# Modulation matrix of a two-layer hybrid diffusion block: one group ahead of the input projection, five through a ring beside attention, in unsplit fp32 products

## What is computed

```python
def reference(x, c, ctx, c_ctx, ada_w, ada_b, norm_w, ...):
    sc, scc = jax.nn.silu(c), jax.nn.silu(c_ctx)
    xc = ctx
    for layer in range(DEPTH):                    # DEPTH = 2
        m = jnp.split((sc @ ada_w[layer] + ada_b[layer])[:, None, :], 6, axis=-1)
        mc = jnp.split(scc @ ada_w[layer] + ada_b[layer], 6, axis=-1)
        nw = norm_w[layer]
        h = modulate(rmsnorm(x, nw[0]), m[0], m[1])       # h * (1 + scale) + shift
        hc = modulate(rmsnorm(xc, nw[0]), mc[0], mc[1])
        y, yc = even_mixer(h, hc, ...) or odd_mixer(h, hc, ...)
        x = x + m[2] * rmsnorm(y, nw[1])
        x = x + m[5] * rmsnorm(ffn(modulate(rmsnorm(x, nw[2]), m[3], m[4])), nw[3])
        # the same for xc with mc, in the first layer alone
    return x
```

## Time and profile before

| what | us |
|---|---|
| median of three runs | 2601.38 |
| lowest, highest | 2595.45, 2602.39 |
| span of the profiled execution | 2596.3 |
| modulation with its columns | 0 to 173.2 |
| norm, up to the first product of the projection | 173.2 to 198.5 |
| input projection | 198.5 to 366 |
| attention jobs | 366 to 476 |

### The profile page before, as it was taken

How to read it: one execution, slowest core, us unless ns; L and a number is a source line. 1 busy time by engine, 2 the same in 40 slices (tenths; PEclk the granted TensorE clock), 3 DMA queues, 4 the chain that set the end, 5 groups by cost and what they waited for, 6 DMA issues and landing times. The chain is left out here.

```text
span 2596.3 us, 29102 instructions
## 1 busy us (share of the span) xinstructions
PE 2334.5 (90%) x11454; PEld 1842.6 (71%) x11454; DVE 1607.9 (62%) x1534; ACT 1205.4 (46%) x1247; POOL 241.4 (9%) x200
## 2 busy tenths in 40 slices
PE   5979999799976999897897759999999999999995
PEld 1338855589865888786755647888888887888884
DVE  5972238453474222233437657888888888888884
ACT  4642222322223222223314326777677777777763
POOL 0000028032410000000034100000000000000000
PEclk9989986899988999998888869999999999999998
DMA  8962210000012333122200128999999999999993
GB/s 316 379 234 80 92 40 1 15 1 1 1 66 78 85 97 98 49 97 97 83 1 1 65 98 304 355 360 348 360 337 361 349 358 330 359 349 345 363 356 128
DMA packets 254976, 482.51 MB, mean 186 GB/s; under 512 B 11314, under 2 KB 80107, under 8 KB 254587
## 3 DMA queue, kind: packets, MB, share of 16 engines
q1 hardware_dynamic: 254703, 478.59, 52.5%
q0 software_dynamic: 144, 2.10, 0.2%
HBM read 479.57 MB, written 1.08 MB: 185 GB/s over the span
## 5 line engine op out<-in xcount | busy, mean ns | idle before, releaser
L134 DVE TENSOR_TENSOR arena_r<-arena,arena_r 128x2048 fp32r<-128x2048 f32 (+2 forms) x466 | 958.5, 2068 | 334.4 <-ACT arena_r L130 314.9
L130 ACT ACTIVATE arena_r<-arena 128x2048 fp32r<-128x2048 f32 (+2 forms) x466 | 804.4, 1737 | 355.0 <-DMA arena<-in_moe_w 272.6
L2009 PE MATMUL bank<-arena_r,gate_rows_r 128*128 128x512 f32 x896 | 350.6, 391 | 0.0
L139 PE MATMUL bank<-hT_r,arena_r 128*128 128x512 f32 (+2 forms) x656 | 254.4, 388 | 37.0 <-DVE arena_r L134 37.0
L2007 PE MATMUL bank<-arena_r,arena_r 128*128 128x512 f32 x672 | 267.0, 397 | 0.0
L2008 PE MATMUL bank<-arena_r,arena_r 128*128 128x512 f32 x672 | 261.5, 389 | 0.0
L140 PE MATMUL bank<-catT_r,arena_r 128*128 128x512 f32 (+2 forms) x656 | 253.8, 387 | 0.0
L141 PE MATMUL bank<-hT_r,arena_r 128*128 128x512 f32 (+2 forms) x656 | 253.4, 386 | 0.0
L2043 PE MATMUL bank<-arena_r,hT_r 128*128 128x512 f32 x448 | 185.7, 414 | 11.6 <-DVE catT_r L2187 11.6
L2009 PEld LDWEIGHTS bank<-arena_r,gate_rows_r 128*128 128x128 f32 x896 | 169.0, 189 | 36.3
L2044 PE MATMUL bank<-arena_r,hT_r 128*128 128x512 f32 x448 | 175.5, 392 | 0.0
(11 more groups left out here) (361 smaller groups left out, 3626.3 us busy)
## 6 DMA issues: line engine op xcount, KB each, us to landing
arena<-in_moe_w SPq DMA_DIRECT2D x336, 1024.0 KB, 5.3
arena<-in_ada_w SPq DMA_DIRECT2D x48, 1024.0 KB, 5.3
arena<-in_ffn_w SPq DMA_DIRECT2D x44, 512.0 KB, 5.2
arena<-in_ev_w_in SPq DMA_DIRECT2D x14, 1024.0 KB, 5.3
arena<-in_ffn_w SPq DMA_DIRECT2D x11, 1024.0 KB, 4.8
arena<-in_od_w_in SPq DMA_DIRECT2D x9, 1024.0 KB, 5.2
arena<-in_ev_w_out SPq DMA_DIRECT2D x4, 1024.0 KB, 8.6
arena<-in_od_w_out SPq DMA_DIRECT2D x4, 1024.0 KB, 8.1
```

Source lines behind the costliest of these rows:

```text
L130: return act.activation(rounded(hi), v, ACT.Copy)
L134: return dve.tensor_tensor(rounded(v), v, rounded(hi).bitcast(F32), ALU.subtract)
L139: pe.matmul(acc, xh_, wh_, start=start, stop=False)
L2009: mm = pe.matmul(out_bank, lo, wh[:, k, :], start=False, stop=(kk == KD - 1))
```

## The change

The six parts of each layer's matrix are taken as three groups of 2048 columns, so six groups of 8 MB in all, each in eight slots of 128 rows by 2048 columns (1 MB). Group 0 is loaded into the arena ahead of the input projection and multiplied there. The other five go through three buffers in `G` (`RING`): three loads are issued at the end of the projection, and 37 beside the attention, each after the product that frees its buffer. Splitting is dropped: a slot is multiplied in plain fp32, in four products of 512 columns whose outputs lie in partitions 0 to 31, 32 to 63, 64 to 95 and 96 to 127 of bank 7. The stationary operand is padded with zeros to 32 columns. VectorE adds the bias rows (`stage`), TensorE turns the whole bank with four transposes, and VectorE writes `modc` and the gate rows of the group. In the attention the eight slots of a group follow jobs 6n to 6n + 4 (two, two, two, one, one), and the turns job 6n + 5. Between two groups SP also writes the gate rows and loads the next bias and norm rows. The first norm's squares, scaling and 28 of its turns are moved ahead of group 0's products; the gate rows are spread into `G` during a later block. The constants are loaded behind seven small loads, and x and ctx ahead of the matrix.

```diff
-        NSLOT, NCH = 6, 24
-        AW = [cut(i * 2048, 4, 512) for i in range(NSLOT)]
-        AWH = ([cut((NSLOT + i) * 2048, 4, 512) for i in range(2)] + [hT[:, 2:6, :]]
-               + [G[:, 2 * i:2 * i + 2, :].rearrange("p a (b n) -> p (a b) n", b=2) for i in range(3)])
...
+        ONE = 2048
+        FIRST = [cut(k * ONE, ONE) for k in range(KD)]
+        RING = [G[:, 2 * i:2 * i + 2, :].rearrange("p a n -> p (a n)") for i in range(3)]
+        GROUPS = [(l, g) for l in range(2) for g in range(3)]
+        n_deferred = (len(GROUPS) - 1) * KD
+        MODS = {0: ((0, 0), (1, 1)), 1: ((1, 2),), 2: ((0, 3),)}
+        GATES = {1: (0, 1, 0), 2: (1, 3, 1)}
+        stage, abias, anorm = sb("ada_stage", [P, 512]), sb("ada_bias_rows", [P, 512]), sb("ada_norm_rows", [P, 512])
+        scP = small[:, 384:640].rearrange("p (k m) -> p k m", k=KD)
...
+        def ada_load_slot(sp, m):
+            n, k = divmod(m, KD)
+            l, g = GROUPS[n + 1]
+            if m >= 3:
+                sp.wait_ge(s_au, KD + m - 2)
+            sp.dma_start(RING[m % 3], adaw[l][:, k, g * ONE:g * ONE + ONE]).then_inc(s_ring[m % 3], 16)
...
+        def ada_store_gates(sp, n):
+            l, g = GROUPS[n]
+            if g in GATES:
+                half, _, which = GATES[g]
+                sp.wait_ge(s_mg, ada_gates_made(n))
+                for jj in range(2):
+                    j = 2 * half + jj
+                    sp.dma_start(gate_dram[l, which, :, jj * 512:jj * 512 + 512], stage[32 * j:32 * j + 2, :]).then_inc(s_g_out, 16)
+
+        def ada_product(pe, slot, k):
+            for j in range(4):
+                mm = pe.matmul(bank[7][32 * j:32 * j + 32, :], scP[:, k, :], slot[:, 512 * j:512 * j + 512], start=(k == 0), stop=(k == KD - 1))
+            mm.then_inc(s_au, 1)
+
+        def ada_slot(pe, m):
+            n, k = divmod(m, KD)
+            if k == 0:
+                pe.wait_ge(s_am, n + 1)
+            pe.wait_ge(s_ring[m % 3], 16 * (m // 3) + 16)
+            ada_product(pe, RING[m % 3], k)
+
+        def ada_turn(pe, n):
+            pe.wait_ge(s_ast, n + 1)
+            for b in range(4):
+                mm = pe.transpose(bank[7][:, b * P:b * P + P], stage[:, b * P:b * P + P], ident)
+            mm.then_inc(s_at, 1)
+
+        def ada_stage_rows(dve, n):
+            dve.wait_ge(s_au, KD * (n + 1))
+            dve.wait_ge(s_ab, ada_bias_landed(n))
+            if n and ada_gates_made(n - 1):
+                dve.wait_ge(s_g_out, 32 * ada_gates_made(n - 1))
+            dve.tensor_tensor(stage[:, :], bank[7][:, :], abias[:, :], ALU.add).then_inc(s_ast, 1)
...
+        def ada_cols(dve, n):
+            l, g = GROUPS[n]
+            dve.wait_ge(s_at, n + 1)
+            turned = bank[7][:, :].rearrange("p (m j c) -> p j m c", m=4, j=4)
+            for half, j in MODS[g]:
+                of = turned[:, 2 * half:2 * half + 2, :, :]
+                if j % 2 == 0:
...
+            ins.then_inc(s_am, 1)
+            if g in GATES:
+                dve.tensor_tensor(stage[:, :], stage[:, :], anorm[:, :], ALU.mult).then_inc(s_mg, 1)
+
+        n_group_jobs = 6
+        ada_slots_at = {n_group_jobs * n + d: [KD * n + s for s in ss]
+                        for n in range(len(GROUPS) - 1) for d, ss in enumerate(((0, 1), (2, 3), (4, 5), (6,), (7,)))}
+
+        def ada_pe_beside(pe, it):
+            for m in ada_slots_at.get(it, ()):
+                ada_slot(pe, m)
+            n, d = divmod(it, n_group_jobs)
+            if d == n_group_jobs - 1 and n + 1 < len(GROUPS):
+                ada_turn(pe, n + 1)
+
+        def ada_dve_beside(dve, it):
+            n, d = divmod(it, n_group_jobs)
+            if n + 1 < len(GROUPS):
+                if d == n_group_jobs - 2:
+                    ada_stage_rows(dve, n + 1)
+                elif d == n_group_jobs - 1:
+                    ada_cols(dve, n + 1)
+
+        def ada_sp_beside(sp):
+            for m in range(3, n_deferred):
+                ada_load_slot(sp, m)
+                n, k = divmod(m - 2, KD)
+                if k == KD - 1:
+                    ada_store_gates(sp, n + 1)
+                    if n + 2 < len(GROUPS):
+                        sp.wait_ge(s_ast, n + 2)
+                        ada_load_bias(sp, n + 2)
+            ada_store_gates(sp, len(GROUPS) - 1)
...
+        def load_in(sp, c):
+            sp.dma_start(WR[c % NWR], WIN[:, :, c * 256:c * 256 + 256]).then_inc(s_wi0[c % NWR], 16)
...
                 sp.dma_start(X[:, 2:4, :], t["ctx"].rearrange("(t p) d -> p t d", p=P)).then_inc(s_x, 16)
+                for k in range(KD):
+                    sp.dma_start(FIRST[k], adaw[0][:, k, 0:ONE]).then_inc(s_first[k], 16)
+                    if k == 3:
+                        sp.wait_ge(s_zero, 1)
+                        ada_load_bias(sp, 0)
+                for c in range(NWR):
+                    load_in(sp, c)
+                sp.dma_start(wg[:, :, :], WIN[:, :, 3584:3600]).then_inc(s_wg, 16)
...
-                def chunk(i, first):
-                    for s in range(NSLOT):
-                        b, h = divmod(s, 2)
-                        if not first and h == 0:
-                            pe.wait_ge(s_row, 3 * i + (b - 2))
-                        pe.wait_ge(s_al, NSLOT * i + (s + 1))
-                        for k in range(4):
-                            kk = 4 * h + k
-                            mm = split_matmul(pe, bank[b][0:2, :], (scTh[:, kk, :], scT[:, kk, :]), (AWH[s][:, k, :], AW[s][:, k, :]), kk == 0, kk == KD - 1)
-                        mm.then_inc(s_ada, 1)
-                chunk(0, True)
-                with pe.Fori(1, NCH // 3) as i:
...
+                def turn(k):
+                    for i in range(4):
+                        if k == 0:
+                            pe.wait_ge(s_xa, i // 2 + 1) if i % 2 == 0 else pe.wait_ge(s_xv, 1 + (i + 1) // 2)
+                        mm = pe.transpose(bank[k][:, i * P:(i + 1) * P], xn0[:, i, k * P:(k + 1) * P], ident)
+                    mm.then_inc(s_tp, 1)
+                pe.wait_ge(s_trc, 1)
+                for k in range(KD - 1):
+                    turn(k)
+                pe.wait_ge(s_sc, 2)
+
+                for k in range(KD):
+                    pe.wait_ge(s_first[k], 16)
+                    ada_product(pe, FIRST[k], k)
+                ada_turn(pe, 0)
+                pe.wait_ge(s_am, 1)
+                turn(KD - 1)
 
...
-                def chunk(i, first):
-                    for b in range(3):
-                        for s in (2 * b, 2 * b + 1):
-                            dve.wait_ge(s_ah, NSLOT * i + (s + 1))
-                            low(dve, AW[s], AWH[s]).then_inc(s_al, 1)
-                        if not (first and b == 0):
-                            dst = add_row(3 * i + (b - 1), NSLOT * i + 2 * b)
-                            dve.tensor_tensor(dst, dst, bank[(b - 1) % 3][0:2, :], ALU.add).then_inc(s_row, 1)
...
+                dve.wait_ge(s_r, 1)
+                for i in (1, 3):
+                    dve.tensor_scalar(xn0[:, i, :], X[:, i, :], r0[:, i:i + 1], None, ALU.mult).then_inc(s_xv, 1)
+                dve.wait_ge(s_trc, 1)
+                dve.wait_ge(s_zero, 1)
+                ada_stage_rows(dve, 0)
+                ada_cols(dve, 0)
+                dve.wait_ge(s_am, 1)
+                for k in range(1, KD, 2):
+                    dve.wait_ge(s_tp, k + 1)
+                    for v in range(2):
+                        ins = dve.tensor_scalar(catT[:, k, 256 * v:256 * v + 256], bank[k][:, 256 * v:256 * v + 256],
+                                                scale0[:, k, v:v + 1], shift0[:, k, v:v + 1], ALU.mult, ALU.add)
+                    ins.then_inc(s_vd, 1)
+                for k in range(KD):
+                    dve.wait_ge(s_hh, k + 1)
+                    low(dve, catT[:, k, :], hT[:, k, :])
...
-                def chunk(i):
-                    for s in range(NSLOT):
-                        act.wait_ge(s_slot[s], 16 * i + 16)
-                        high(act, AWH[s], AW[s]).then_inc(s_ah, 1)
...
+                if sp_beside:
+                    @block.sync
+                    def _(sp):
+                        sp_beside(sp)
...
+                        if pe_beside and j < n_jobs:
+                            pe_beside(pe, j)
...
-        def in_ahead(sp):
-            load_in(sp, 0)
-
-            for n, (l, j, v) in enumerate(((0, 0, 0), (0, 1, 0), (1, 0, 0), (1, 1, 0), (0, 0, 1), (0, 1, 1))):
-                sp.dma_start(G[:, n, :], gate_dram[l, j, v:v + 1, :].to_broadcast([P, D])).then_inc(s_g_in, 16)
-            for c in range(1, NWR):
-                load_in(sp, c)
-            sp.wait_ge(s_g_in, 96)
-            sp.dma_start(wg[:, :, :], WIN[:, :, 3584:3600]).then_inc(s_wg, 16)
-        norm_to_hT("l0_mix", 0, 0, range(4), cut(8192, 4, D), ahead=in_ahead)
...
+                ada_load_bias(sp, 1)
                 for c in range(NWR, WCH):
                     sp.wait_ge(s_pj, made[c - NWR])
```

(32 more changed lines are left out.)

181 lines of the change are left out of this document (77 added, 104 removed).

## The result

The changed kernel takes **2501.5 us** (median; 2499.1 to 2504.7) against 2598.6 of the kernel before measured with it: ratio 0.9631, 95% interval 0.9616 to 0.9646. That is 97 us gained; the forecast was 86.5, the time 2515. The profiled execution has a span of 2499.1 us against 2596.3.

What follows compares the result with a forecast made beforehand. It took an all-DMA modulation front ahead of two stretches without DMA work as the bound. Front -141.9 plus attention +55.4 gave -86.5 us: span 2510, median 2515 us, own range 2500 to 2535.

Steps and rivals of the forecast that it cites:

- both terms: Front up to the first projection product: 141.9 us gained; attention with 40 MB of deferred loads and products: 55.4 us given back.
- rival (b): Slots in front and attention: all four blocks run at once, 0.86 us a slot, 2496 us in total; chance 0.08.
- Arrival and norm: Front: loads 2.71 us per MB, ctx at 15.1, eighth slot landed at 36.8, norm turns done at 26.8 us.
- The slot: Four fp32 products per 1 MB slot: neighbouring products overlap only in pairs of passes, 1.71 us; bounds 3.43 and 0.86.
- The sum of the front: Front: eight slots end at 40.5 us, modulation at 42.8, projection starts at 56.6 instead of 198.5, 141.9 us gained.
- Context groups: Attention groups beside context jobs: the ring of loads, not TensorE, sets them, 28.7 us each (28.5 for the first).
- The third load's place in SP's queue: Each new group's third load waits behind gates and up to eight small issues, landing about 9 us after the columns.
- Latent groups: Attention groups beside latent jobs: TensorE sets them, 33.1 us against the ring's 28.7; 33.5 and 34 in the sum.
- The clock: TensorE in the attention: the added dense passes bring full clock after a first 4 us.
- Rival (c): Attention: TensorE's clock stays at its lower level, 187 us given back, 2646 us; chance 0.08, alone or with unoverlapped slots.
- Sum: Attention: groups, two jobs and the pipeline's end total 165.7 us against 110.3 before, 55.4 us given back.

Runs made afterwards that it cites:

- run 7: Changed kernel with a group's gate stores and bias loads queued on SP behind the sixth load of the next group instead of the second: 2489.5 us, ratio 0.9599.
- run 4: Changed kernel with all products kept but no loads after the ring's first three: 2474.9 us, attention 126.9 us.
- runs 3: Changed kernel with the ring loads kept but one product of two columns in place of each attention slot's four: 2510.2 us, attention 165.9 us.
- three small edits: Changed kernel with a fourth ring slot, gate stores and bias loads behind the next group's sixth load, and neighbourhood bias loaded in the projection: 2468.3 us, ratio 0.9508.

## Why the prediction was right, and where it was wrong

The direction, the size and the place of both terms held: the front gained, the attention gave back. The time came out 13.5 us under the forecast, next to rival (b), for which I had given 0.08. That it still lies in my own range, 1.5 us above its low end, is luck: the 4.4 us lost behind the attention, which the forecast didn't have, are more than that, and the waits for the neighbourhood bias, left out as well, made up for part of the slot.

- *Arrival and norm.* ctx was there at 14.4 us (15.1 forecast), the turns ran to 26.4 (26.8). Right. The eighth slot was awaited until 34.55, where I had 36.8: the loads came some 2.5 us apart, not 2.71.
- **The slot was mis-sized: 1.71 us forecast, 0.89 measured.** The step that failed is the reading of the earlier trace rows. That two passes on one block don't overlap was right: with one block a slot takes 3.46 us. What I added, that the next product's first pass has to wait for the second pass of the product ahead, was wrong: four passes start within 21 ns, and since passes on one block don't run together, they are one of each block. The earlier trace rows couldn't show it. There eight passes on one block stand ahead of eight on the other, and one pass is saved at the boundary. I took the one pass that I saw for the most that there is. What the row allowed was a bound from below, not a price. One place of the kernel before does show alternating neighbours, and I overlooked it: the scores of the first three jobs, which follow each other with contraction rows 0 to 63 and 64 to 127 in turn (line 486). The whole row, and then the same view of what is running at 366.53 us:

```profile
366.51 1.10 PE L495 MATMUL bank<-arena 64*128 64x256 f32 x6 [1.39 <-PEq L628]
```

```profile
366.51 0.49 PE L495 MATMUL bank<-arena 64*128 64x256 f32 x2 [1.39 <-PEq L628]
```

The single records start at 366.515, 366.522, 366.806, 366.842, 367.022 and 367.238: the first passes of the first two products together, then their second passes together, then the third product's two passes alone. So a second pass doesn't hold the first pass of the next product. These products differ in their contraction rows, and those of a slot in the partitions that they write, so the row is evidence against my model and not a price for the slot.

- *The sum of the front.* Products end at 35.6 instead of 40.5, the rest took 15.8 us instead of 16.1 (the 13.8 us from modulation to projection were exact). 147.0 us gained instead of 141.9.
- *Context groups.* That the ring, not TensorE, sets them, was right: 26.5 and 27.6 us with loads (28.5 and 28.7 forecast), 21.0 and 21.6 without. (That isn't TensorE's own 16.0 either, 8.5 + 8 x 0.86 + 0.6: without loads it waits 5.22 us for VectorE at the end of group 1.) The third load's place in SP's queue was the cause I gave, and run 7 confirms it. The columns of group 1 are made at 248.0 (line 236 in VectorE's order of time), and the third slot starts at 255.97, 8 us on; I had 9. In the first group, though, the ring was late for a reason that I had left out: the bias load of 2 MB beside it, 7.38 us of waiting.
- *Latent groups.* Set by TensorE, as forecast, with the wrong slot: 33.5 forecast and 27.3 measured for group 4, and 33.1 less eight times 0.82 is 26.5, what the run without loads has. Group 5 took 33.3, near the 34 forecast, but by other causes: SP's order, and the clock of 0.89. Without them it takes 27.0 (run 4) to 27.6 (run 7).
- *The clock.* I took full clock after 4 us, where the row that I took it from gives 5.7 (479.9 to 485.6), and to the end. It was 0.82, 0.77 and 0.93 in the first three stretches. Rival (c), a low clock throughout, didn't happen, and runs 3 and 4 show why: the slots' own dense passes raise it.
- *Sum.* 44.9 us given back instead of 55.4, 0.6 more between the projection's first product and the first scores (168.6 us against 168.0), and the 4.4 us lost later, which the forecast didn't have: -147.0 + 0.6 + 44.9 + 4.4 = -97.1, with the spans 97.2 apart.

The Trainium skill, "TensorEngine Tiling (Array Packing)", Theoretical Speedup, gives up to 4x where a dimension is at most 32, and its Key Properties say that tiles operate independently. The runs agree: 3.46, 1.74 and 0.89 us for one, two and four blocks. The Trainium skill's Key Properties there also say that changing the tiling mode drains TensorE. The runs agree that a change of shape has a price, a small one. Without loads, the latent group 5 takes 26.95 us, and six jobs of 3.14, eight slots of 0.86 and the turns of 0.6 add up to 26.3; the rest is 0.13 for each of the five places where slots stand between jobs. One such place, of two slots, takes 315.17 - 313.32 = 1.85 us instead of 1.72:

```profile
313.32 1.92 PE L206 MATMUL bank<-gate_rows,small 128*32 128x512 f32 x16
315.17 1.12 PE L592 MATMUL bank<-arena 64*128 64x512 f32 x2
```

In the single records of that run the last PV pass (128x64) starts at 301.128 and the first slot pass (128x32) at 301.330, 0.20 us on, where PV passes stand 0.11 apart; the bias product and the turns, both 128x128, follow each other without such a step. Whether it is a drain that takes the 0.09 us, no run sets apart.

## What to carry to other kernels

fp32 products with few weight columns can be issued to four 32-column blocks in turn, so that a weight stream with two rows costs TensorE a quarter; price such an overlap by a run, since a row in which the blocks don't alternate can't show it. When loads move beside a stage that idles the DMA, list every load of that stage and every small transfer in the same queue: here three small edits together gave back 33 us, 22 of them in the attention; alone, two of them gained 12 and 15 us and one nothing that could be shown. Extra dense TensorE work can pay for part of itself through the clock, so don't charge it at full price against a stage that runs at half clock.

## What the runs showed of the hardware

- fp32 products of 512 columns, 128 rows: a pass starts every 0.43 us on one block, two passes 7 ns apart every 0.43 us on two blocks, four within 21 ns every 0.43 to 0.46 us on four, with 32 weight columns and with 2.
- Taking TensorE work out of the attention made it slower: 165.9 us with 40 small products in place of 40 slots (granted clock 0.50 in the stretches from 247 to 303 us), 152.9 with the slots (0.77 to 1.00).
- Slots put between jobs cost 0.13 us per place beyond their passes (26.95 us for a latent group whose parts add up to 26.3).
- A 2 MB load beside the ring delayed one 1 MB slot by 4.8 us (7.38 against 2.57 to 2.61).
